# Loads and side work of a one-core transformer trunk's first projection, put in another order

## The reference

```
def adaln(cond, w_mod, b_mod):
    m = jax.nn.silu(cond) @ w_mod + b_mod
    return jnp.split(m, 6, axis=-1)

def modulate(x, shift, scale):
    return x * (1.0 + scale) + shift
...
qr, kr, vr, gr, qn, kn, vn = _split(h @ w_in, EVEN_SIZES)      # h = modulate(x), w_in (1024, 3072)
...
log_gamma = jax.nn.log_sigmoid(decay_logit)                    # 8 decays of the retention heads
intra = where(rel >= 0, exp(lg * max(rel, 0)), 0)              # decay matrices
s_ctx = einsum('bhqd,blhd->bhql', qr, kc) * scale              # kc, vc: cached keys and values
```

## Time and profile before

| | us |
|---|---|
| median of 3 runs | 1196.08 (1192.82 to 1197.23) |
| the profiled execution | 1196.54, its span 1194.4 |
| TensorE busy | 1083.5 of the span |
| first product of u0 | starts at 46.07 |

### The profile page before, as it was taken

How to read it: one execution, slowest core, us unless ns; L and a number is a source line. 1 busy time by engine, 2 the same in 40 slices (tenths; PEclk the granted TensorE clock), 3 DMA queues, 4 the chain that set the end, 5 groups by cost and what they waited for, 6 DMA issues and landing times.

```text
span 1194.4 us, 30538 instructions
## 1 busy us (share of the span) xinstructions
PE 1083.5 (91%) x12866; PEld 711.9 (60%) x12866; DVE 537.7 (45%) x1122; ACT 403.0 (34%) x764; POOL 51.7 (4%) x85
## 2 busy tenths in 40 slices
PE   3699897899999999999985987789999999999993
PEld 1589786555555555555544987665555555555541
DVE  1433665444434444334337484545443443444435
ACT  3433323233333333223225453323333333333331
POOL 2100010000000000110000101000000000000000
PEclk9799997999999999999996988799999999999997
DMA  9995855599999997554416743529999999600000
GB/s 330 354 333 191 309 206 212 190 394 409 408 408 408 408 407 283 181 218 171 144 37 211 190 168 117 212 103 391 408 408 408 408 408 408 268 2 2 2 2 36
DMA packets 106079, 303.24 MB, mean 254 GB/s; under 512 B 9132, under 2 KB 40012, under 8 KB 105944
## 3 DMA queue, kind: packets, MB, share of 16 engines
q1 hardware_dynamic: 94176, 262.17, 57.4%
q0 software_dynamic: 10576, 37.20, 9.0%
q10 hardware_dynamic: 1192, 1.92, 0.4%
HBM read 500.06 MB, written 2.52 MB: 421 GB/s over the span
## 4 chain that ended last, share of the span: by engine, by line
PE 86%; DVE 6%; DMA 4%; ACT 2%; issue 1%; SPq 1%; DVEq 0%; ACTq 0%
PE ps L1544 83%; DMA slab<-in_w_mod 4%; PE ps L1547 4%; DVE temp L1202 1%; DVE small L1204 1%; DVE temp L1201 1%; DVE slab L1057 0%; ACT temp L886 0%; ACT hi_main L761 0%; SPq L605 0%; SPq L517 0%; DVE slab L1313 0%; DVE x_tok L1228 0%; ACT slab L892 0%; DVE temp L1226 0%
## 5 line engine op out<-in xcount | busy, mean ns | idle before, releaser
L1544 PE MATMUL ps<-slab 128*32 128x256 f32 (+2 forms) x7792 | 544.8, 423 | 3.3 <-DVE slab L1313 2.0
L1544 PEld LDWEIGHTS ps<-slab 128*32 128x32 f32 (+1 forms) x7792 | 262.2, 111 | 268.2 <-issue 148.1
L1406 DVE SCALAR_TENSOR_TENSOR o_lo<-ps,ex,o_hi 128x512 fp32r<-128x512 f32 x192 | 143.9, 751 | 176.3 <-ACT o_hi L930 171.6
L930 ACT ACTIVATE o_hi<-ps,ex 128x512 fp32r<-128x512 f32 x192 | 132.2, 688 | 209.5 <-PE ps L1544 198.8
L920 ACT ACTIVATE slab<-ps 128x128 f32<-128x128 f32 x96 | 26.6, 277 | 269.5 <-PE ps L1544 269.5
L1389 DVE TENSOR_TENSOR ex<-slab,ps 128x128 f32<-128x128 f32 x96 | 27.5, 287 | 190.3 <-ACT slab L920 190.3
L1544 PE MATMUL ps<-pick_at,x_hi 128*128 128x256 f32 x384 | 106.9, 311 | 0.7 <-ACT slab L892 0.4
L1013 DVE TENSOR_TENSOR lo_main<-slab,hi_main 128x2048 fp32r<-128x2048 f32 x30 | 68.7, 2291 | 81.0 <-ACT hi_main L761 77.0
L1544 PEld LDWEIGHTS ps<-pick_at,x_hi 128*128 128x128 f32 x384 | 72.0, 188 | 39.6 <-issue 36.7
L1544 PE MATMUL ps<-pick_at,x_lo 128*128 128x256 f32 x384 | 95.6, 281 | 0.0
L1313 DVE COPY slab<-ps 128x512 f32<-128x512 f32 x96 | 66.4, 692 | 61.6 <-PE ps L1544 61.6
(11 more groups left out here) (234 smaller groups left out, 1015.4 us busy)
## 6 DMA issues: line engine op xcount, KB each, us to landing
slab<-in_exp_w_gate SPq DMA_DIRECT2D x256, 512.0 KB
slab<-in_exp_w_up SPq DMA_DIRECT2D x256, 512.0 KB
slab<-in_exp_w_down SPq DMA_DIRECT2D x256, 512.0 KB
slab<-in_w_mod SPq DMA_DIRECT2D x24, 1024.0 KB, 10.1
slab<-in_w_in_even SPq DMA_DIRECT2D x12, 1024.0 KB, 8.2
slab<-in_w_in_odd SPq DMA_DIRECT2D x10, 1024.0 KB, 6.0
temp<-in_w_mod POOLq DMA_DIRECT2D x8, 1024.0 KB, 5.8
slab<-in_w_mod POOLq DMA_DIRECT2D x8, 1024.0 KB, 6.5
```

Source lines behind the costliest of these rows:

```text
L930: nc.scalar.activation(o_hi[:, c * 512:(c + 1) * 512], ps[:, 6 + c, :], ACT.Copy, scale=slot_gate[:, j % 2:j % 2 + 1]).then_inc(o_hi_out, 1)
L1406: V.scalar_tensor_tensor(out=o_lo[:, cols], in0=ps[:, 6 + c, :], scalar=slot_gate[:, j % 2:j % 2 + 1], in1=o_hi[:, cols].bitcast(F32), op0 ...
L1544: return nc.tensor.matmul(out, w, x, start=start, stop=stop)
```

## The change

Six things move; one piece of memory is used in another's place.

- **Constants in two pieces.** The table is ordered anew, so that the first 139 columns (unit matrix, ones, epsilons, fold) are all that is loaded at the start; the other 800 columns, the decay logits and `early` are issued by ScalarE behind its `hi_main_of` for u1 (`late_loads`). `early` lies in `next_third` now, a buffer that is free in this stage, instead of in `proj`; with that the wait of `unit_copy` for `k_dec_ready` at u0 goes.
- **Caches.** POOL's loads of cached keys, values and state, and the write of the padded table behind them, wait for `main_used` 9 (u0 multiplied) instead of 5 (m4 multiplied).
- **Tokens.** TensorE transposes them behind m3 instead of behind m6.
- **Decays.** ScalarE's first step (three operations on 12 columns) stands behind its copy of u1, its second (12 exponentials and a small one) behind its copy of u2; VectorE's steps stand behind the differences for u3 and u5.
- **Cached keys.** TensorE transposes them behind u1, ahead of m9, instead of behind m7; ScalarE copies them out behind the second step of the decays, and TensorE waits for that copy behind u3, ahead of m11.
- **New waits.** VectorE and TensorE wait for the 800 columns (`rest_in`) before they first use one.

```diff
@@ pool @@
-            pool.wait_ge(main_used, len(FIRST_MODS) - MOD_RAW)
+            pool.wait_ge(main_used, len(FIRST_MODS) + 1)
             pool.dma_start(kc_in, A["cache_na_k"][0, 0]).then_inc(cache_k_in, 16)
@@ scalar @@
-            act.dma_start(const[:, :], A["shape_consts"][:, 0:KEPT_N]).then_inc(consts_in, 16)
...
+            act.dma_start(const[:, 0:FIRST_N], A["shape_consts"][:, 0:FIRST_N]).then_inc(consts_in, 16)
             act.dma_start(bias_rows, A["b_mod"].rearrange("l (s n) -> (l s) n", s=6)).then_inc(mod_bias_in, 16)
-            act.dma_start(early, A["shape_consts"][:, KEPT_N:EARLY_END]).then_inc(early_in, 16)
...
+            def late_loads():
...
+                act.dma_start(early, A["shape_consts"][:, KEPT_N:EARLY_END]).then_inc(early_in, 16)
+                act.dma_start(const[:, FIRST_N:], A["shape_consts"][:, FIRST_N:KEPT_N]).then_inc(rest_in, 16)
...
                 for n in range(IN_UNITS[l]):
                     split_to(in_unit(l, n + 1) if n + 1 < IN_UNITS[l] else out_unit(l, 0))
+                    if l + n == 0:
+                        late_loads()
                     unit_copy(l, n)
+                    if l == 0 and n in (1, 2):
+                        decays(n - 1)
+                    if l == 0 and n == 2:
+                        act.wait_ge(cache_t, 1)
+                        nc.scalar.activation(kc_t, ps[:, 7, :].rearrange("p (h t) -> p h t", h=H), ACT.Copy) \
+                            .then_inc(cache_t_out, 1)
@@ vector @@
                     split_to(in_unit(l, n + 1) if n + 1 < IN_UNITS[l] else out_unit(l, 0))
...
+                    if l == 0 and n in (2, 4):
+                        decays(n // 2 - 1)
@@ tensor @@
-                    mods(FIRST_MODS[:5])
-                    section_fold(0)
-                    mods(FIRST_MODS[5:7])
+                    mods(FIRST_MODS[:4])
                 x_turned(l, 0)
                 if l == 0:
-                    mods(FIRST_MODS[7:])
...
+                    section_fold(0)
+                    mods(FIRST_MODS[4:])
                     section_fold(1)
```

More of the change, by code:

```diff
@@ L160 @@
     LOADED.append(_at[_s % RAW])
-KEPT = dict(ident=128, cos=64, sin=64, window=128, one=1, ln_eps=1, rms_eps=1, fold=4 * 2,
+KEPT = dict(ident=128, one=1, ln_eps=1, rms_eps=1, fold=4 * 2, cos=64, sin=64, window=128,
             before=128, lower=128, number=128, job=64, job_rank=64, slot=32)
@@ L176 @@
 KEPT_AT, KEPT_N = columns(KEPT)
+FIRST_N = KEPT_AT["cos"][0]
 EARLY_AT, EARLY_END = columns(EARLY, KEPT_N)
@@ L279, in build @@
         ln_feat = K("window")[:, 0:2 * 2 * DEPTH * KC].rearrange("p (w n k) -> p w n k", w=2, k=KC)
-        early = part(PROJ_AT, EARLY_N)
+        early = next_third[:, :, :].rearrange("p a n -> p (a n)")[:, 0:EARLY_N]
         def E(name):
@@ L784, in _ @@
             nc.scalar.activation(cond_s[:, :, :], cond[:, :, :], ACT.Silu).then_inc(cond_ready, 1)
[L787 to L800, removed]
@@ L801, in _ @@
-            act.wait_ge(decay_ready, 16)
-            nc.scalar.activation(small[:, 0:8], small[:, 8:16], ACT.Exp).then_inc(decay_ready, 1)
+            def late_loads():
+                logit = decay[:, 0:12]
+                flat = A["ret_decay_logit"].rearrange("a d h -> a (d h)")
+                act.dma_start(logit[:, 0:8], flat.partition_broadcast(P)).then_inc(decay_in, 16)
+                for d in range(2):
+                    act.dma_start(logit[d * DK:(d + 1) * DK, 8:12],
+                                  A["ret_decay_logit"][:, d].partition_broadcast(DK)).then_inc(decay_in, 16)
+                act.dma_start(early, A["shape_consts"][:, KEPT_N:EARLY_END]).then_inc(early_in, 16)
+                act.dma_start(const[:, FIRST_N:], A["shape_consts"][:, FIRST_N:KEPT_N]).then_inc(rest_in, 16)
@@ new lines, in decays @@
+            def decays(step):
+                if step == 0:
+                    act.wait_ge(decay_in, 48)
+                    act.wait_ge(consts_in, 16)
+                    link(nc.scalar.activation(decay[:, 12:24], decay[:, 0:12], ACT.Abs))
+                    link(nc.scalar.activation(decay[:, 24:36], decay[:, 12:24], ACT.Exp, scale=-1.0))
+                    nc.scalar.activation(decay[:, 36:48], decay[:, 24:36], ACT.Ln, bias=K("one")).then_inc(decay_ready, 1)
+                else:
+                    act.wait_ge(decay_ready, 2)
+                    act.wait_ge(early_in, 16)
+                    for d, rel in enumerate(("rel_f", "rel_b")):
+                        for h in range(H):
+                            nc.scalar.activation(dec_e[:, d, h], E(rel), ACT.Exp,
+                                                 scale=decay[:, 48 + 4 * d + h:49 + 4 * d + h]).then_inc(decay_ready, 1)
+                    for h in range(H):
+                        nc.scalar.activation(q_pow[:, h], E("pos_row"), ACT.Exp, scale=decay[:, 56 + h:57 + h]) \
+                            .then_inc(decay_ready, 1)
+                    act.wait_ge(decay_ready, 16)
+                    nc.scalar.activation(small[:, 0:8], small[:, 8:16], ACT.Exp).then_inc(decay_ready, 1)
@@ L841, in unit_copy @@
                 if l == 0 and n == 0:
-                    act.wait_ge(k_dec_ready, 1)
                     b3 = halves
@@ L1080, in normalise, with decays @@
                 V.tensor_tensor(s, s, along(den, keys), ALU.mult).then_inc(probs, 1)
+            def decays(step):
+                if step == 0:
+                    dve.wait_ge(decay_ready, 1)
+                    link(V.tensor_scalar(decay[:, 48:60], decay[:, 0:12], 0.0, None, ALU.min))
+                    V.tensor_tensor(decay[:, 48:60], decay[:, 48:60], decay[:, 36:48], ALU.subtract).then_inc(decay_ready, 1)
+                    dve.wait_ge(decay_ready, 2)
+                    dve.wait_ge(early_in, 16)
+                    for d in range(2):
+                        ins = V.tensor_scalar(small[:, 8 + 4 * d:12 + 4 * d], decay[:, 48 + 4 * d:52 + 4 * d],
+                                              E("pos_col")[:, d:d + 1], None, ALU.mult)
+                        ins.then_inc(decay_ready, 1)
+                else:
+                    dve.wait_ge(decay_ready, 16)
+                    for d, mask in enumerate(("mask_f", "mask_b")):
+                        ins = V.tensor_tensor(dec_e[:, d], dec_e[:, d], over(E(mask), H), ALU.mult)
+                    link(ins)
+                    link(V.tensor_tensor(dmat, dec_e[:, 0], dec_e[:, 1], ALU.add))
+                    dve.wait_ge(decay_ready, 17)
+                    V.memset(small[:, 48:49], 0.0).then_inc(k_dec_ready, 1)
+                    dve.wait_ge(rest_in, 16)
             def softmax_in(l, banks):
@@ L1416, in _ @@
             V.tensor_scalar(raised, raised, 1.0, None, ALU.add).then_inc(mod_bias_ready, 1)
[L1417 to L1425, removed]
             section_rows(0)
             section_out(0)
[L1428 to L1434, removed]
             dve.wait_ge(consts_in, 16)
@@ L1862, in _ @@
                         (by_features if feat else by_tokens)(u, 4 + SPLIT_NO[u] % 2)
-                    if l == 0 and n == 0:
+                    if l == 0 and n == 1:
+                        pe.wait_ge(cache_k_in, 16)
+                        for h in range(H):
+                            ins = turned(head(7, h), kc_in[:, h])
+                        ins.then_inc(cache_t, 1)
+                    if l == 0 and n == 3:
                         pe.wait_ge(cache_t_out, 1)
@@ L1872, in _ @@
                     pe.wait_ge(section_ready, 4)
+                    pe.wait_ge(rest_in, 16)
                     pe.wait_ge(cache_t_out, 1)
```

15 lines of the change are left out of this document (1 added, 14 removed).

## The result

Over 20 runs each the kernel took 1190.82 us where the one before took 1195.82. The ratio of the runs is 0.9951, with a 95% interval of 0.9937 to 0.9965, that is 4.2 to 7.5 us faster. One of the changed kernel's twenty runs took 4686.9 us and is left out of the ratio. The same kernel built again gave 0.9958 (0.9939 to 0.9977). The forecast was 1.7 us.

The account below looks back on a forecast made before the run. Loads were taken to bound the first 53 us, TensorE's projection the time behind; 5.2 us at u0 shrink to 2.4 at m9, less 0.7 for decays, 1.7 us faster: median 1194.4 us, range 1190.2 to 1197.8.

Parts of the forecast that it names:

- 5.5 us taken off the front: Loads ahead of m7: 2.1 us of constants and `early` plus 3.4 us of POOL's queue leave, so m7 lands at 34.1.
- the term of 0.7 us: Decays on ScalarE ahead of u4: `hi_main_of` 0.3 us late, the difference behind it makes 0.7 us late in all.
- The rival with the dearer change of table: ScalarE's decay steps: each table load costs a further 1.3 us, `hi_main_of` for u4 later; 1195.7 us, chance 0.05.
- the granted clock didn't drop inside u2: Sign for the rival that nothing is left: granted clock of 0.50 in u2, after the wait ahead of m9.
- the work ahead of m9's landing is the same as before unless some is still outstanding: Late loads beside u4 and m9: postponed bytes are paid ahead of m9 whatever each queue's share; m9 lands at 58.1.
- only 0.9 us taken as outstanding: Ahead of m9: only the padded table's reading back, 0.9 us, falls behind m9, which lands at 58.1 instead of 59.05.
- the wait of 2.1 us: TensorE ahead of m9: wanted at 56.0, landing at 58.1, so a wait of some 2 us.
- the 2.4 us of gain: At m9: begun at 58.1 instead of 60.50, leaving 2.4 us of the 5.2 us gained at u0.
- no more is lost or won: At m10: wanted at 65.0, landed at 64.7 even before, so the gain left at m9 stays.
- The first: Rival: late loads yield to q1, m9 and m10 in time, 5.2 us less 0.7 kept; 1191.6 to 1190.7 us, chance 0.20.
- Nothing is left: Rival: the wait ahead of m9 lowers the clock, costing 1.6 us, or loads lose in mixing; 1196.0 us, chance 0.22.
- slower: Rival: logits land late, at 18 us after issue, holding ScalarE's `hi_main_of` for u3; 1198.6 us, chance 0.08.

Follow-up runs that it names:

- released at m4: Changed kernel with POOL's loads released when slice m4 is multiplied, as before the change, instead of at u0; ratio to the kernel before 0.9986.
- 512 KB more: Changed kernel with one more useless 512 KB load on POOL's queue behind the state; ratio to the kernel before 0.9957.
- released at 36: Changed kernel with POOL's loads released when m7 is multiplied (near 36 us) instead of u0; ratio to the kernel before 0.9977.
- POOL's later loads held back: Changed kernel with cached values, state and padded table held until m11 (ratio 0.9979), or until m13 with 12 exponentials behind u6, u7, u8 (0.9963).
- the filling that kept the clock up: Useless unit-matrix transposes, 32 ahead of m6 and 20 behind the second fold: on the changed kernel 0.9958, with decays and padded table late 0.9949.
- decays and table late: Changed kernel with 12 exponentials behind u6, u7, u8 and cached values, state, padded table held until m13; ratio to the kernel before 0.9963.
- the other kernel with both late: Changed kernel with decays and padded table late, plus useless transposes ahead of m6 and behind the second fold; ratio to the kernel before 0.9949.

## Why the prediction was wrong

**Right, with their sizes.** m7 at 34.1 (34.04), made slower by the clock (1.93 us), u0 at 40.9 (40.80), m8 at 48.4 without a wait (48.48). So the 5.5 us taken off the front were priced well. The cached keys came in time, with nothing to spare. `hi_main_of` for u4 was to be done 8.25 us behind the start of m10:

```profile
69.17 1.90 ACT L763 ACTIVATE hi_main<-slab 128x2048 fp32r<-128x2048 f32 x1
```

71.07 - 62.91 = 8.16. ScalarE's lateness of 0.3 us at u4 is seen as a wait of 0.30 or 0.31 us in four experiments that had no wait for m11 and the decays in this place. In a fifth, with 512 KB more, the slow clock behind m10 gave ScalarE the time. In the changed kernel it costs nothing in the first profile, because TensorE waits for m11 in the same time, and 0.4 us in the second. So the term of 0.7 us was sized right where nothing hides it: released at m4, it is 0.4 from m11 to u4 and 0.3 from u4 to the mark. The rival with the dearer change of table falls with the 8.16 us. The logits landed 6.7 us behind their issue at most, so that rival falls too, and the granted clock didn't drop inside u2.

**The step that failed** is "the work ahead of m9's landing is the same as before unless some is still outstanding", with only 0.9 us taken as outstanding. m9 was put at 58.1; it was issued at 37.89 and landed 16.6 us later, at 54.5. POOL's queue up to m9's landing, before (0:59.05) and after (0:54.5), as packets, MB and share:

```profile
q0 software_dynamic: 720, 1.54, 10.5%
```

```profile
q0 software_dynamic: 246, 0.52, 5.6%
```

At that time 1.02 MB of POOL's loads had still to come, not only the 0.26 MB of the padded table's reading back (which was issued at 60.19; the forecast had said not before 60). At the forecast's own price, 3.4 us for 1.18 MB, that is 2.9 us instead of 0.9, and m9 would be put at 56.1, where TensorE wanted it. So the wait of 2.1 us was wrong, and with it the 2.4 us of gain: released at 48.85, POOL's loads had only 5.6 us. Shown by experiment: with the same bytes released at 36, m9 comes at 59.19 and the gain at the mark is 0.6 us. The forecast described that kernel as far as m9 (58.1); it had no wait for m8, and gave 1.7 us at u4 where that kernel has 0.95.

The remaining 1.6 us of m9 are a matter of the rate. When m9 landed, all queues had moved 20.20 MB at a mean of 342 GB/s before and 19.11 MB at 351 now. At the old mean the 1.09 MB less are 3.2 us, and the better mean makes 1.4. Two queues at work together don't explain it: 1.39 and 0.50 MB went through in 45:50, 378 GB/s, but SP's queue alone had 374 in 49:54 before, so its 348 is the rate of that stretch and not of one queue. What is gone from ahead of m9 is a slow stretch, in which the padded table was read back. All queues before the change, in 42.65:49 and in 49:54:

```profile
DMA packets 1680, 2.02 MB, mean 318 GB/s; under 512 B 155, under 2 KB 1451, under 8 KB 1679
DMA packets 1238, 1.87 MB, mean 374 GB/s; under 512 B 31, under 2 KB 1031, under 8 KB 1238
```

By an estimate from these two rows it cost (374 - 318) x 6.35 us = 0.36 MB, 0.9 us, beyond its own bytes. The second profile of the kernel before shows it too (324 and 373). That this is most of the 1.4 us is argued, not shown.

**Where the bind went.** The rule that the forecast rested on holds two slices later. m11 was issued at 60.69 before and 55.87 after, and landed 9.7 and 14.5 us later, at 70.4 in both:

```profile
slab<-in_w_mod SPq DMA_DIRECT2D x1, 1024.0 KB, 14.5
```

By 70.4 the queues of SP and POOL had moved, before and after:

```profile
q1 hardware_dynamic: 11426, 20.83, 84.5%
q0 software_dynamic: 720, 1.54, 8.8%
```

```profile
q1 hardware_dynamic: 11438, 20.90, 84.5%
q0 software_dynamic: 720, 1.54, 9.1%
```

Here everything postponed is paid back, and the gain is what m11 had to spare before the change: 74.38 - 70.4 = 4.0 us, 3.9 at u4. In every kernel that moves the same bytes m11 landed between 69.6 and 71.3; with POOL's later loads held back it landed at 65.3 to 65.9. (With 512 KB more it landed at 71.2, but had been issued earlier, at 54.95.) How much the wait for it cost is another matter: 0.6 us in one profile and 0.2 in the other, part of which ScalarE would have taken anyway. I had stopped at m10, where "no more is lost or won", and never worked out m11. The Trainium skill's statement that all issuers' transfers share the 16 engines (DMA: Bandwidth & Descriptors, "Issuing engines are not separate DMA queues") is borne out by these rows; it says nothing on when the debt is due, which was the question.

**The rivals.** The first (late loads yield, 5.2 less 0.7, 1191.6 us) described u0 to m10, was 0.6 us too high at u4, and its time is the nearest to the 1190.82. Its mechanism was not what happened: the late loads did not yield. SP's queue had 105.5% of the 16 engines in 42:45, 76.8% beside ACT's loads in 45:50, and 65.4% beside ACT's and POOL's in 50:54.5. "Nothing is left" and "slower" did not occur.

**Open.** The marks give 3.3 to 3.8 us and the spans 4.2 to 4.6; the medians give 5.0 and the ratio 4.2 to 7.5. From the mark to the end of the span it is 1113.1 and 1110.2 us before and 1112.7 and 1108.9 now. Whether 1 us more comes from the stages behind, where the wait for m20 varies between runs by 1.4 us and the clock with it, these runs don't settle.

## What to carry to other kernels

Taking loads off a bound start pays at once, but the bytes come back as a debt. Find the first load that lands after all of the postponed ones, and take its slack as the limit of the gain; a slice that is wanted sooner sees only what was released long enough before it. Holding the postponed work back further moves the bind to a later load, or removes it where the DMA engines have idle time; here that was worth something only together with the filling that kept the clock up. Check whatever is then issued late and waited for soon, as with the cached keys here.

## What was not expected of the hardware

A wait of only 0.69 us was followed by a fall of the granted clock. In the kernel with decays and table late, TensorE waits for the copy of the last unit, works 2.2 us, and then, in the middle of work, the clock goes from 1.00 to 0.50, 1.2 GHz, for about three microseconds. Its timeline and windows (the last three columns are clock, DMA share and GB/s):

```profile
125.95 2.05 PE L1566 MATMUL ps<-slab 64*128 64x128 f32 x16 [0.69 <-ACT slab L867]
...
128.17 3.65 PE L1566 MATMUL ps<-slab 128*128 128x128 f32 x16
```

```profile
128.00:129.00 1.00, 1.00 (x8) 0.93 (x7) 0.88 (x3) 0.00 (x0) 0.00 (x0) 0.67 1.01 393
129.00:130.00 1.00, 1.00 (x7) 1.00 (x6) 1.00 (x4) 0.00 (x0) 0.00 (x0) 0.50 1.02 406
```

The same 16 products took 2.05 us, behind the same wait of 0.69 us, in all twelve profiles of the other kernels. It cost 1.6 us, and it was there in the other kernel with both late as well (3.53 us for the 16 products; 6.7 us from this wait to m16, where others have 5.1). Both are the kernels that hold loads until m13, so it may go with the order of the work and not with the wait; what sets it off was not tried.
